# A state space stage whose output rotation goes from VectorE to GpSimd

## The chip, the core and the metric

One core of a Trainium2 chip runs the whole program. The metric is the device time of one execution in microseconds; where several runs are given, their median. Beside the times there is one profiled execution of the same kernel, and all rows below come from it.

## The reference

The program computes two transformer-like blocks one after the other on a sequence of 256 tokens of width 2048, in f32. The change touches one part of the second block, the state space layer:

```python
def s5_ssm(u, a_re, a_im, log_dt, b_re, b_im, c_re, c_im, d_skip):
    # 32 groups of 16 channels, 64 complex states for each group
    bu_re = jnp.einsum('gph,blgh->blgp', bb_re, ug)
    bu_im = jnp.einsum('gph,blgh->blgp', bb_im, ug)
    # combine: complex product of a decay and a state, plus the new input
    _, _, xs_re, xs_im = lax.associative_scan(combine, (a_re_t, a_im_t, bu_re, bu_im), axis=1)
    y = (jnp.einsum('ghp,blgp->blgh', c_re, xs_re)
         - jnp.einsum('ghp,blgp->blgh', c_im, xs_im)
         + d_skip.reshape(SSM_GROUPS, SSM_GROUP) * ug)
```

The result goes through a gelu, a gated linear unit and a branch product, and is merged with a windowed attention branch through sigmoid gates.

## The kernel before

**Weight products.** Nearly all of the time goes into products of a stationary weight tile with 256 tokens. Each f32 weight is split into a high part (ScalarE, L379) and a low part (VectorE, L473: raw minus high), and TensorE multiplies high by high, high by low and low by high (L670, L671, L672). A chunk is four weight tiles of 128x256, 512 KB; a ring of four chunks holds raw, high and low parts. SyncE loads chunk c when the low part of chunk c-4 is made; ScalarE and VectorE make chunk c's parts when TensorE is done with chunk c-4 and the load has landed; TensorE takes 24 matmuls for a chunk. A unit of four chunks fills one PSUM bank, which VectorE evacuates (L543 in this stage) before the unit after next is due; ScalarE then applies the sigmoid (L433).

**The state space stage.** It runs while TensorE computes the 40 chunks of the gates (phase `ps`). A complex state decays by its magnitude and turns by its angle at each token. The kernel takes the turning out: it multiplies the input by a table of rotations (the cosines `er` and sines `ei` of `s_tab`), runs a real scan with the magnitude alone, and rotates the scanned states back. The states are worked in four quarters `q` of four tiles, each quarter in two halves `p` of two tiles, so eight halves of 128x512 elements for a real and an imaginary part (`xr`, `xi`). For each half VectorE in `StateSpace.dve` does, in this order:

- input rotation, L2502 to L2510: four multiplies of a table (SBUF) with the product that TensorE left in PSUM (`work`), one add, one subtract (both inputs in SBUF);
- four scans of 128x256, L2514 (two inputs in SBUF);
- output rotation, L2521 to L2528: four multiplies, one subtract and one scalar_tensor_tensor, all in SBUF, with temporaries `tq`, `sq` and `ta`; the last one computes `-q3 - q1`, the negated imaginary part, which the output product needs.

Between these steps stand calls of `split()`. Each makes as many low splits of gate chunks as are due by its count (`4 * EACH * calls // 64`, with eight calls a half), so that TensorE gets weights in step. After the first half of quarters 1 to 3 VectorE also adds the skip term to the output of the quarter before (`output`, L2460), for which it waits for TensorE's output sum.

**TensorE in the stage.** Before certain chunks it computes the inputs of a half (`inputs`, before chunks 9q-1 and 9q+2) or the output sum of a quarter (`outputs`, L2438, 16 matmuls, before chunk 9q+13; the last one after chunk 39). `outputs(q)` waits for `made`, which VectorE raises after a quarter's second output rotation. The next table load into the same slot waits for that output sum, as do the scans that overwrite its states.

**GpSimd.** Its queue is one list: tables of the state space in the first block (`StateTables.pool_factors`, `pool_tables`), low parts and sums of squares of the phases, then two instructions for the attention (`window.pool`), then the later phases. The output matrix `gi` of the tables is the imaginary part that multiplies `xi`.

The order on each engine is written out by hand; no planner moves anything.

Of the kernel before, what the change touches and what calls it, by code (L numbers as in the profile page):

```python
# [22 lines left out]
ALU = mybir.AluOpType  # L23
# [3 lines left out]
T = 256  # L27
# [38 lines left out]
QT = ST // 4  # L66
# [124 lines left out]
class Stream:  # L191
# [402 lines left out]
    def pool(self, eng, phs):  # L594
        for ph in phs:
            if ph.k.pool:
                def step(v, j, ph=ph):
                    self.pool_finish(eng, ph, v, (ph.base["u"] + j) % 2)
                self.loop(eng, ph, step)
# [1349 lines left out]
class StateTables:  # L1949
# [71 lines left out]
    def pool_factors(self, eng):  # L2021
        link, em, sqs, s = self.link, self.em, self.sqs, self.s
        tt, ts = eng.tensor_tensor, eng.tensor_scalar
        abr, abi, zr, zi, t1, den = self.abr, self.abi, self.zr, self.zi, self.t1, self.den
        are, aim = s.par("are"), s.par("aim")
        eng.memset(self.tab[:, :, S5_C:S5_M], 0.0)
        eng.wait_ge(self.waves, 1)
        eng.wait_ge(self.inverse, 1)
        eng.tensor_copy(em[:, 0, 0, :], self.co[:])
        link(eng.tensor_copy(em[:, 0, 1, :], self.si[:]))  # L2030
        for n in range(7):
            c, sn = em[:, n, 0, :], em[:, n, 1, :]
            tt(sqs[:, 0, :], c, c, ALU.mult)
            tt(sqs[:, 1, :], sn, sn, ALU.mult)
            link(tt(em[:, n + 1, 1, :], c, sn, ALU.mult))
            tt(em[:, n + 1, 0, :], sqs[:, 0, :], sqs[:, 1, :], ALU.subtract)
            link(ts(em[:, n + 1, 1, :], em[:, n + 1, 1, :], 2.0, None, ALU.mult))
        tt(abr[:], self.mag[:], self.co[:], ALU.mult)
        link(tt(abi[:], self.mag[:], self.si[:], ALU.mult))
        link(ts(abr[:], abr[:], -1.0, None, ALU.add))  # L2040
        for z, x, y, op in ((zr, abr, abi, ALU.add), (zi, abi, abr, ALU.subtract)):
            tt(z[:], x[:], are, ALU.mult)
            link(tt(t1[:], y[:], aim, ALU.mult))
            link(tt(z[:], z[:], t1[:], op))
            link(tt(z[:], z[:], den[:], ALU.mult))
        eng.wait_ge(self.loaded, 32)
        zrw, ziw = spread(zr[:], 16), spread(zi[:], 16)
        for g, x, y, op in ((self.gr, self.cr, self.ci, ALU.subtract), (self.gi, self.ci, self.cr, ALU.add)):
            tt(g[:], x[:], zrw, ALU.mult)
            link(tt(self.tmp[:], y[:], ziw, ALU.mult))  # L2050
            link(tt(g[:], g[:], self.tmp[:], op))

    def pool_tables(self, eng, half):
        link, em, w1, w2 = self.link, self.em, self.w1, self.w2
# [299 lines left out]
class StateSpace:  # L2354
# [5 lines left out]
    def __init__(self, dram, s, ua, pa, gates, window, states, tab, xr, xi, bq, sem):  # L2360
        self.dram, self.s, self.ua, self.pa, self.gates, self.window = dram, s, ua, pa, gates, window
        self.states, self.tab, self.xrs, self.xis, self.bq = states, tab, xr, xi, bq
        self.q1, self.q2, self.q3 = s.tq[:], s.sq[:], s.ta[:]
        self.inputs_in = [sem("even_inputs_loaded"), sem("odd_inputs_loaded")]
        self.tables_in = [sem("even_states_loaded"), sem("odd_states_loaded")]
        (self.lk, self.bu, self.bu_read, self.made, self.summed, self.mixed, self.gelu, self.high,
         self.low) = (sem("space_" + n) for n in (
             "vector_link", "bu_ready", "bu_read", "ready", "outputs_summed", "outputs_mixed", "gelu_ready",
             "outputs_high", "outputs_low"))

    def bank(self, i):
# [56 lines left out]
        ins.then_inc(self.bu, 1)  # L2428

    def outputs(self, eng, q):  # L2430
        eng.wait_ge(self.made, q + 1)
        if q < 2:
            eng.wait_ge(self.window.low, q + 3)
        at_least(eng, self.mixed, q - 1)
        for b in range(QT):
            for im, xs in ((0, self.xrs[q % 2]), (1, self.xis[q % 2])):
                at = S5_C + (im * QT + b) * P
                ins = eng.matmul(self.ybank(q), self.tab[:, q % 2, at:at + P], xs[:, b, :],  # L2438
                                 start=b + im == 0, stop=b == QT - 1 and im == 1)
        ins.then_inc(self.summed, 1)  # L2440
# [10 lines left out]
    def dve_last(self, eng):  # L2451
# [3 lines left out]
        eng.tensor_tensor(s.a0[:, 0:4, 1, :], self.ua[:, S2:S2 + 4, :], s.a0[:, 0:4, 0, :].bitcast(F32),  # L2455
                          ALU.subtract).then_inc(self.low, 1)

    def output(self, eng, q):
        eng.wait_ge(self.summed, q + 1)
        eng.scalar_tensor_tensor(out=self.ua[:, S2 + q, :], in0=self.ua[:, S2 + q, :], scalar=self.s.par("d2", q),  # L2460
                                 in1=self.ybank(q), op0=ALU.mult, op1=ALU.add).then_inc(self.mixed, 1)

    def dve(self, eng, previous):
        s, gates = self.s, self.gates
        link = Link(eng, self.lk)
        tt, stt = eng.tensor_tensor, eng.scalar_tensor_tensor
        q1, q2, q3 = self.q1, self.q2, self.q3
        chunks = gates.units * gates.nc
        done, calls = [0], [0]

        def one():

            v, k = divmod(done[0], gates.nc)
            s.split_low(eng, gates, v, v, k)
            if k == gates.nc - 1:
                if v:
                    s.evacuate(eng, gates, v - 1, (gates.base["u"] + v - 1) % 2)
                else:
                    s.evacuate(eng, previous, previous.units - 1, (gates.base["u"] - 1) % 2)
            done[0] += 1  # L2480

        def split():

            calls[0] += 1
            while done[0] < min(chunks, self.LEAD + 4 * self.EACH * calls[0] // 64):
                one()

        for _ in range(self.LEAD):
            one()
        for q in range(4):  # L2490
            er, ei = (self.tab[:, q % 2, S5_E + k * QT * T:S5_E + (k + 1) * QT * T].rearrange("p (a t) -> p a t", a=QT)
                      for k in range(2))
            xr, xi = self.xrs[q % 2], self.xis[q % 2]
            eng.wait_ge(self.tables_in[q % 2], 16 * (q // 2 + 1))
            for p in range(2):
                split()
                eng.wait_ge(self.bu, 2 * q + p + 1)
                if q > 1 and p == 0:
                    eng.wait_ge(self.summed, q - 1)
                pr = slice(2 * p, 2 * p + 2)  # L2500
                re, im = (self.bank(2 * p + i).rearrange("p (a t) -> p a t", a=2) for i in range(2))
                tt(q1, er[:, pr], re, ALU.mult)  # L2502
                link(tt(q2, ei[:, pr], im, ALU.mult))  # L2503
                split()
                link(tt(xr[:, pr], q1, q2, ALU.add))  # L2505
                tt(q1, er[:, pr], im, ALU.mult)
                split()
                tt(q2, ei[:, pr], re, ALU.mult).then_inc(self.bu_read, 1)
                eng.wait_ge(self.bu_read, 2 * q + p + 1)
                link(tt(xi[:, pr], q1, q2, ALU.subtract))  # L2510
                split()
                for jl in range(2 * p, 2 * p + 2):
                    for xs in (xr, xi):
                        ins = eng.tensor_tensor_scan(  # L2514
                            xs[:, jl, :], self.tab[:, q % 2, S5_M + jl:S5_M + jl + 1].to_broadcast([P, T]),
                            xs[:, jl, :], 0.0, ALU.mult, ALU.add)
                    if jl % 2 == 0:
                        split()
                link(ins)
                split()  # L2520
                tt(q1, er[:, pr], xr[:, pr], ALU.mult)  # L2521
                tt(q3, ei[:, pr], xr[:, pr], ALU.mult)  # L2522
                link(tt(q2, ei[:, pr], xi[:, pr], ALU.mult))  # L2523
                split()
                link(tt(xr[:, pr], q1, q2, ALU.subtract))
                link(tt(q1, er[:, pr], xi[:, pr], ALU.mult))
                split()
                ins = stt(out=xi[:, pr], in0=q3, scalar=-1.0, in1=q1, op0=ALU.mult, op1=ALU.subtract)  # L2528
                if p == 0:
                    link(ins)  # L2530
                    if q:
                        self.output(eng, q - 1)
                else:
                    ins.then_inc(self.made, 1)
                    eng.wait_ge(self.made, q + 1)
        while done[0] < chunks:
            one()


def feed_forwards(nc, dram, s, a1, fo, raw, out_dram, states):  # L2540
    with ExitStack() as st:
# [68 lines left out]
        with nc.Block() as block:  # L2610
# [60 lines left out]
            def _(eng):  # L2671
# [7 lines left out]
                s.pool(eng, ffn[6:])  # L2679
                tables.stores_done(eng)  # L2680
                window.pool(eng)
                s.pool(eng, phs)

            @block.tensor
# [221 lines left out]
```

## Time and profile before

| | us |
|---|---|
| median of 3 runs (lowest, highest) | 2882.45 (2881.48, 2887.85) |
| span of the profiled execution | 2882.9 |
| TensorE busy | 2802.8 (97%) |
| VectorE busy | 1823.4 (63%) |
| ScalarE busy | 1245.7 (43%) |
| GpSimd busy | 396.0 (14%) |

The profile gives the span from the first to the last instruction; the execution's own time is not given beside it, and the span stands for it. Busy shares are averages over stages with different limits, so the rows for single stretches matter more. A matmul's end is modelled: its row shows 0.28 us while the next one starts 0.11 us after it. A time in a row of the timeline counts from the start of the span.

### The profile page before, as it was taken

To read this page: it belongs to the slowest core of one execution; us is meant where nothing else is said; L and a number is where in the kernel's file an instruction comes from. 1 tells how busy PE (TensorE), PEld (TensorE's weight loads), DVE (VectorE), ACT (ScalarE), POOL (GpSimd) and SP (SyncE) were. 2 spreads that over 40 slices of the span, in tenths; PEclk is the share of its full clock that TensorE was granted. 3 is DMA by queue.
4 is the path that set the end of the run, shared out by engine and by line. 5 is a ranking of instruction groups with operands and counts; after the bars stand their busy time and mean duration, and the time that the engine had idled before them with its cause. 6 is when DMAs were issued, how large, how long until landed. Compare 5 with 4: busy or idle time off the path is not lost.

```text
span 2882.9 us, 61146 instructions
## 1 busy us (share of the span) xinstructions
PE 2802.8 (97%) x24650; PEld 2752.2 (95%) x24650; DVE 1823.4 (63%) x2175; ACT 1245.7 (43%) x1511; POOL 396.0 (14%) x549
## 2 busy tenths in 40 slices
PE   8999699999999999999999999999999999999998
PEld 8999687999989999999999999998999999999998
DVE  6678747775435655655555668697667655665664
ACT  5355223544334543444434545434454443443444
POOL 0000230110002139300461210000110000010011
PEclk9999899999999999999999999999999999999999
DMA  6654002566635566666667565554555665556564
GB/s 235 195 192 147 16 31 88 191 189 204 190 102 164 190 197 190 219 213 189 197 194 236 191 195 163 193 196 157 193 192 189 197 192 193 193 188 199 184 198 149
DMA packets 138418, 514.10 MB, mean 178 GB/s; under 512 B 15360, under 2 KB 15616, under 8 KB 136960
## 3 DMA queue, kind: packets, MB, share of 16 engines
q1 hardware_dynamic: 138240, 511.58, 54.9%
q8 instruction: 129, 2.11, 0.3%
q14 instruction: 49, 0.40, 0.0%
HBM read 503.12 MB, written 8.40 MB: 177 GB/s over the span
## 4 chain that ended last, share of the span: by engine, by line
PE 64%; DVE 4%; issue 1%; ACT 1%; DVEq 0%; ACTq 0%
PE acc L670 21%; PE acc L671 21%; PE acc L672 21%; DVE lo L473 1%; PE work L2170 0%; ACT hi L379 0%; DVE s_xr L2514 0%; PE acc L2203 0%; DVE tb L543 0%; DVE sq L2523 0%; DVE ua L2514 0%; DVE ub L2514 0%; DVE s_xr L2505 0%; DVE sq L2503 0%; DVE ta L2522 0%
## 5 line engine op out<-in xcount | busy, mean ns | idle before, releaser
L670 PE MATMUL acc<-a,hi 128*128 128x256 f32 x5504 | 1527.0, 277 | 16.3 <-DVE lo L473 14.5
L671 PE MATMUL acc<-a,hi 128*128 128x256 f32 x5504 | 1521.5, 276 | 0.0
L672 PE MATMUL acc<-a,lo 128*128 128x256 f32 x5504 | 1521.4, 276 | 0.0
L473 DVE TENSOR_TENSOR lo<-qx,hi 128x1024 fp32r<-128x1024 f32 x704 | 896.4, 1290 | 674.6 <-ACT hi L379 672.9
L670 PEld LDWEIGHTS acc<-a,hi 128*128 128x128 f32 x5504 | 1035.3, 188 | 20.5 <-issue 14.8
L671 PEld LDWEIGHTS acc<-a,hi 128*128 128x128 f32 x5504 | 1035.3, 188 | 0.8 <-issue 0.5
L672 PEld LDWEIGHTS acc<-a,lo 128*128 128x128 f32 x5504 | 1035.3, 188 | 0.0
L379 ACT ACTIVATE hi<-qx 128x1024 fp32r<-128x1024 f32 x704 | 733.9, 1057 | 646.4 <-PE acc L672 629.0
L620 POOL TENSOR_TENSOR a<-th,a 128x512 f32 (+1 forms) x64 | 84.9, 1327 | 1381.2 <-ACT a L424 1381.1
L473 DVE TENSOR_TENSOR lo_x<-next_raw,hi_x 128x1024 fp32r<-128x1024 f32 x128 | 162.2, 1281 | 115.0 <-ACT hi_x L379 115.0
L670 PE MATMUL acc<-a,hi_in 128*128 128x256 f32 x768 | 215.4, 280 | 9.8 <-DVE lo_in L473 9.8
L670 PE MATMUL acc<-a,hi_x 128*128 128x256 f32 x768 | 215.8, 281 | 5.8 <-DVE lo_x L473 5.8
L672 PE MATMUL acc<-a,lo_in 128*128 128x256 f32 x768 | 213.8, 278 | 0.0
L671 PE MATMUL acc<-a,hi_in 128*128 128x256 f32 x768 | 213.8, 278 | 0.0
L671 PE MATMUL acc<-a,hi_x 128*128 128x256 f32 x768 | 212.8, 277 | 0.0
L672 PE MATMUL acc<-a,lo_x 128*128 128x256 f32 x768 | 212.8, 277 | 0.0
L379 ACT ACTIVATE hi_x<-next_raw 128x1024 fp32r<-128x1024 f32 x128 | 133.9, 1058 | 144.2 <-PE acc L672 94.9
L473 DVE TENSOR_TENSOR lo_in<-raw_in,hi_in 128x1024 fp32r<-128x1024 f32 x96 | 115.4, 1222 | 68.2 <-ACT hi_in L379 68.1
L670 PEld LDWEIGHTS acc<-a,hi_in 128*128 128x128 f32 x768 | 146.1, 190 | 11.2 <-DVE lo_in L473 9.7
L670 PEld LDWEIGHTS acc<-a,hi_x 128*128 128x128 f32 x768 | 144.9, 189 | 8.5 <-issue 5.8
L671 PEld LDWEIGHTS acc<-a,hi_in 128*128 128x128 f32 x768 | 146.0, 190 | 0.3 <-issue 0.2
L672 PEld LDWEIGHTS acc<-a,lo_in 128*128 128x128 f32 x768 | 145.9, 190 | 0.0
(503 smaller groups left out, 2779.2 us busy)
## 6 DMA issues: line engine op xcount, KB each, us to landing
qx<-in_ffn SPq DMA_DIRECT2D x256, 512.0 KB, 4.2
raw_in<-in_w_in SPq DMA_DIRECT2D x96, 512.0 KB, 4.3
qx<-in_w_in SPq DMA_DIRECT2D x92, 512.0 KB, 3.7
qx<-in_up_gate SPq DMA_DIRECT2D x88, 512.0 KB, 4.2
qx<-in_up_val SPq DMA_DIRECT2D x88, 512.0 KB, 4.3
qx<-in_down SPq DMA_DIRECT2D x88, 512.0 KB, 4.2
next_raw<-in_wq SPq DMA_DIRECT2D x32, 512.0 KB, 4.3
next_raw<-in_wk SPq DMA_DIRECT2D x32, 512.0 KB, 4.3
```

The lines of the kernel that those rows point to most:

```text
L379: eng.activation(self.hi[:, slot, :], self.raw[:, slot, :], ACT.Copy).then_inc(self.s_hi, 1)
L473: eng.tensor_tensor(self.lo[:, slot, :], self.raw[:, slot, :], self.hi[:, slot, :].bitcast(F32), ALU.subtract).then_inc(self.s_lo, 1)
L620: eng.tensor_tensor(out[:, :, 1, :], self.th[:, s], out[:, :, 0, :].bitcast(F32), ALU.subtract).then_inc(self.s_pool, 1)
L670: eng.matmul(out, self.hi[:, slot, cols], a[:, 0, :], start=opens, stop=False)
L671: eng.matmul(out, self.hi[:, slot, cols], a[:, 1, :], start=False, stop=False)
L672: ins = eng.matmul(out, self.lo[:, slot, cols], a[:, 0, :], start=False, stop=closes)
```

## The change

The output rotation of seven halves moves to GpSimd. A new `StateSpace.pool`, placed in GpSimd's queue behind the attention's two instructions, waits for a half's scans (`scanned`), rotates in place and raises `turned`. The eighth half is rotated by VectorE, behind its last two `split()` calls. The new `turn` holds six instructions: four multiplies (two into temporaries, two in place), a subtract and an add. GpSimd's temporaries are `sq2` and `ta`, VectorE's `tq` and `sq`. The imaginary part is no longer negated; instead `gi` is multiplied by -1 once, when the tables are made. TensorE's output sum waits for `turned` (two for each quarter; for the last one 7, and `made` of VectorE). VectorE no longer waits for `made` in its loop, has six `split()` calls a half and 50 in all, and the divisor goes from 64 to 50.

```diff
@@ StateTables.pool_factors
             link(tt(g[:], g[:], self.tmp[:], op))
+        link(ts(self.gi[:], self.gi[:], -1.0, None, ALU.mult))
@@ StateSpace.__init__
-        self.q1, self.q2, self.q3 = s.tq[:], s.sq[:], s.ta[:]
+        self.q1, self.q2 = s.tq[:], s.sq[:]
+        self.p1, self.p2 = s.sq2[:], s.ta[:]
@@ StateSpace.outputs
-        eng.wait_ge(self.made, q + 1)
+        if q < 3:
+            eng.wait_ge(self.turned, 2 * q + 2)
+        else:
+            eng.wait_ge(self.turned, 7)
+            eng.wait_ge(self.made, 1)
@@ new in StateSpace
+    def turn(self, eng, link, q, p, v1, v2):
+        er, ei = self.factors(q)
+        pr = slice(2 * p, 2 * p + 2)
+        xr, xi = self.xrs[q % 2][:, pr], self.xis[q % 2][:, pr]
+        tt = eng.tensor_tensor
+        tt(v1, ei[:, pr], xr, ALU.mult)
+        tt(v2, ei[:, pr], xi, ALU.mult)
+        tt(xr, er[:, pr], xr, ALU.mult)
+        link(tt(xi, er[:, pr], xi, ALU.mult))
+        tt(xr, xr, v2, ALU.subtract)
+        return tt(xi, xi, v1, ALU.add)
+
+    def pool(self, eng):
+        link = Link(eng, self.plk)
+        for n in range(7):
+            eng.wait_ge(self.scanned, n + 1)
+            self.turn(eng, link, n // 2, n % 2, self.p1, self.p2).then_inc(self.turned, 1)
+            eng.wait_ge(self.turned, n + 1)
@@ StateSpace.dve
-            while done[0] < min(chunks, self.LEAD + 4 * self.EACH * calls[0] // 64):
+            while done[0] < min(chunks, self.LEAD + 4 * self.EACH * calls[0] // 50):
...
-                link(ins)
+                ins.then_inc(self.scanned, 1)
                 split()
-                tt(q1, er[:, pr], xr[:, pr], ALU.mult)
-                tt(q3, ei[:, pr], xr[:, pr], ALU.mult)
-                link(tt(q2, ei[:, pr], xi[:, pr], ALU.mult))
-                split()
-                link(tt(xr[:, pr], q1, q2, ALU.subtract))
-                link(tt(q1, er[:, pr], xi[:, pr], ALU.mult))
-                split()
-                ins = stt(out=xi[:, pr], in0=q3, scalar=-1.0, in1=q1, op0=ALU.mult, op1=ALU.subtract)
-                if p == 0:
-                    link(ins)
-                    if q:
-                        self.output(eng, q - 1)
-                else:
-                    ins.then_inc(self.made, 1)
-                    eng.wait_ge(self.made, q + 1)
+                if p == 0 and q:
+                    self.output(eng, q - 1)
+        eng.wait_ge(self.scanned, 8)
+        split()
+        split()
+        self.turn(eng, link, 3, 1, q1, q2).then_inc(self.made, 1)
@@ GpSimd's queue
                 window.pool(eng)
+                space.pool(eng)
                 s.pool(eng, phs)
```

## Rows read from the trace of the kernel before

**Rows 1.** The page, part 1: busy us (share of the span) xinstructions.

```profile
PE 2802.8 (97%) x24650; PEld 2752.2 (95%) x24650; DVE 1823.4 (63%) x2175; ACT 1245.7 (43%) x1511; POOL 396.0 (14%) x549
```

**Rows 2.** Busy us by engine in the stage: start:end, length, engines, granted clock.

```profile
1835.00:1973.00 138.00, 130.89 (x1045) 126.59 (x1044) 129.88 (x176) 47.46 (x66) 0.00 (x0) 1.00 0.52 169
```

**Rows 3.** Waits of TensorE, 1831 to 1980: us in total, times, longest.

```profile
PE acc L670 <- DVE lo L473: 7.1, 8, 1.3
```

**Rows 4.** Timeline of TensorE: start us, us, instruction, idle time before.

```profile
1870.99 0.28 PE L672 MATMUL acc<-a,lo 128*128 128x256 f32 x1
1872.08 0.36 PE L670 MATMUL acc<-a,hi 128*128 128x256 f32 x1 [0.82 <-DVE lo L473]
1872.28 0.28 PE L671 MATMUL acc<-a,hi 128*128 128x256 f32 x1
```

**Rows 5.** Timeline of VectorE, first output rotation to the next split.

```profile
1847.78 0.68 DVE L2521 TENSOR_TENSOR tq<-s_tab,s_xr 128x512 f32<-128x512 f32 x1
...
1851.16 1.23 DVE L473 TENSOR_TENSOR lo<-qx,hi 128x1024 fp32r<-128x1024 f32 x1
```

**Rows 6.** Groups of VectorE, 1831 to 1973: count, busy us, mean ns, idle before.

```profile
L473 DVE TENSOR_TENSOR lo<-qx,hi 128x1024 fp32r<-128x1024 f32 x38 | 46.4, 1221 | 7.8 <-ACT hi L379 7.0
L2514 DVE TENSOR_TENSOR_SCAN s_xr<-s_tab,s_xr 128x256 f32<-128x256 f32 x16 | 10.9, 680 | 0.1
...
L2528 DVE SCALAR_TENSOR_TENSOR ub<-ta,tq 128x512 f32<-128x512 f32 x4 | 2.7, 683 | 0.0
```

**Rows 7.** Groups of GpSimd, whole span.

```profile
L614 POOL TENSOR_TENSOR sq<-sq,tq 128x512 f32<-128x512 f32 x27 | 35.2, 1305 | 231.5 <-ACT tq L421 231.5
```

**Rows 8.** Timeline of GpSimd and VectorE, a table step in the first block.

```profile
1111.45 1.04 POOL L2069 TENSOR_TENSOR t_w<-t_tab,t_em 128x512 f32<-128x512 f32 x1
1112.05 1.52 DVE L473 TENSOR_TENSOR lo<-qx,hi 128x1024 fp32r<-128x1024 f32 x1 [1.28 <-ACT hi L379]
1112.45 2.02 POOL L2070 TENSOR_TENSOR t_w<-t_tab,t_em 128x512 f32<-128x512 f32 x1
1113.49 0.68 DVE L496 TENSOR_TENSOR x<-acc,x 128x512 f32 x1
1114.55 1.30 POOL L2071 TENSOR_TENSOR t_tab<-t_w 128x512 f32<-128x512 f32 x1
1114.77 2.16 DVE L473 TENSOR_TENSOR lo<-qx,hi 128x1024 fp32r<-128x1024 f32 x1 [0.59 <-ACT hi L379]
...
1119.88 1.29 POOL L2074 TENSOR_TENSOR t_tab<-t_w 128x512 f32<-128x512 f32 x1
```

**Rows 9.** Timeline of VectorE: first instruction of the halves 4 and 6.

```profile
1889.92 0.68 DVE L2502 TENSOR_TENSOR tq<-s_tab,work 128x512 f32<-128x512 f32 x1
...
1923.07 0.68 DVE L2502 TENSOR_TENSOR tq<-s_tab,work 128x512 f32<-128x512 f32 x1
```

**Rows 10.** Timeline of VectorE, end of the last output rotation.

```profile
1971.30 0.68 DVE L543 TENSOR_TENSOR tb<-acc,rstd 128x512 f32<-128x512 f32 x1
1971.90 0.68 DVE L2528 SCALAR_TENSOR_TENSOR ua<-ta,tq 128x512 f32<-128x512 f32 x1
```

**Rows 11.** The chain that ended last, by time: TensorE's last output sum.

```profile
1974.61 3.45 PE acc L2438 x16
```

**Rows 12.** Half 4's rotation begins; second output sum; TensorE's waits 1835 to 1908.

```profile
1899.34 0.69 DVE L2521 TENSOR_TENSOR tq<-s_tab,s_xr 128x512 f32<-128x512 f32 x1
1908.17 0.59 PE L2438 MATMUL acc<-s_xr,s_tab 128*128 128x256 f32 x2
PE acc L670 <- DVE lo L473: 2.0, 2, 1.2
```

**Rows 13.** Timeline of GpSimd in the first block.

```profile
1087.00 0.74 POOL L2051 TENSOR_TENSOR t_gi<-t_gi,t_tmp 128x256 f32<-128x256 f32 x1
...
1213.57 1.30 POOL L620 TENSOR_TENSOR a<-th,a 128x512 f32 x1 [9.60 <-ACT a L424]
```

**Rows 14.** Busy us by engine behind the stage, columns as in rows 2.

```profile
2055.00:2065.00 10.00, 8.18 (x58) 7.98 (x58) 7.96 (x9) 4.90 (x6) 2.83 (x2) 0.84 0.50 184
```

**Rows 15.** Groups of ScalarE, 1831 to 1973.

```profile
L433 ACT ACTIVATE ub<-tb,prm 128x256 f32<-128x256 f32 x18 | 8.2, 503 | 79.4 <-DVE tb L543 79.4
```

More of the change, by code:

```diff
@@ L2362, in __init__ @@
         self.states, self.tab, self.xrs, self.xis, self.bq = states, tab, xr, xi, bq
-        self.q1, self.q2, self.q3 = s.tq[:], s.sq[:], s.ta[:]
+        self.q1, self.q2 = s.tq[:], s.sq[:]
+        self.p1, self.p2 = s.sq2[:], s.ta[:]
         self.inputs_in = [sem("even_inputs_loaded"), sem("odd_inputs_loaded")]
         self.tables_in = [sem("even_states_loaded"), sem("odd_states_loaded")]
-        (self.lk, self.bu, self.bu_read, self.made, self.summed, self.mixed, self.gelu, self.high,
-         self.low) = (sem("space_" + n) for n in (
-             "vector_link", "bu_ready", "bu_read", "ready", "outputs_summed", "outputs_mixed", "gelu_ready",
+        (self.lk, self.plk, self.bu, self.bu_read, self.scanned, self.turned, self.made, self.summed, self.mixed,
+         self.gelu, self.high, self.low) = (sem("space_" + n) for n in (
+             "vector_link", "pool_link", "bu_ready", "bu_read", "scanned", "turned", "last_turned", "outputs_summed", "outputs_mixed", "gelu_ready",
              "outputs_high", "outputs_low"))
@@ L2456, in dve_last, with factors @@
                           ALU.subtract).then_inc(self.low, 1)
+    def factors(self, q):
+        return (self.tab[:, q % 2, S5_E + k * QT * T:S5_E + (k + 1) * QT * T].rearrange("p (a t) -> p a t", a=QT)
+                for k in range(2))
+    def turn(self, eng, link, q, p, v1, v2):
[15 more added lines that the diff above has]
+            eng.wait_ge(self.turned, n + 1)
     def output(self, eng, q):
@@ L2466, in dve @@
         tt, stt = eng.tensor_tensor, eng.scalar_tensor_tensor
-        q1, q2, q3 = self.q1, self.q2, self.q3
+        q1, q2 = self.q1, self.q2
         chunks = gates.units * gates.nc
@@ L2490, in dve @@
         for q in range(4):
-            er, ei = (self.tab[:, q % 2, S5_E + k * QT * T:S5_E + (k + 1) * QT * T].rearrange("p (a t) -> p a t", a=QT)
-                      for k in range(2))
+            er, ei = self.factors(q)
             xr, xi = self.xrs[q % 2], self.xis[q % 2]
```

## The prediction

> **What bounds the kernel now.** I began with the page: TensorE is busy 97% of the span and GpSimd 14% [rows 1], so a gain can come only where TensorE waits. The busy times by stretch then show the state space stage of the second block as the odd one: from 1835 to 1973 us VectorE is busy 129.9 of 138 us, TensorE 130.9, GpSimd never, at full clock [rows 2]. The waits of TensorE in that stage are one kind: for the low part of a weight chunk, which VectorE makes, 7.1 us in 8 waits [rows 3]. No wait there ends on a transfer or on ScalarE. So VectorE bounds the stage, by little.
>
> The 7.1 us understates the loss. A gap is counted from the modelled end of the last matmul, 0.28 us after its start, while running matmuls start every 0.11 us. Around the first stall the starts are 1.09 and 0.20 us apart instead of 0.11 and 0.11: 1.07 us lost where the wait says 0.82 [rows 4]. At 0.25 us more for each of eight, the stage loses 7.1 + 2.0 = 9.1 us. This is the ceiling of the gain here.
>
> **What the change removes from VectorE.** Seven of eight output rotations, six instructions each. The first five of one take 1851.16 - 1847.78 = 3.38 us start to start [rows 5]; the sixth has the same form, mean 0.68 [rows 6]. Together 4.06 us, seven times: 28.4 us. The other work stays: 36 low splits, 32 scans, the input rotation. The new divisor, 50, fits the six split calls that a half now has (6 x 8 + 2), so the splits stay evenly spread, 4.3 a half against 4.5.
>
> **What it adds to GpSimd.** 42 multiplies, subtracts and adds of 128x512 f32. One alone takes 1.30 us [rows 7]; GpSimd has nothing else in the stage [rows 2]. Six of exactly this kind, two multiplies and a sum twice over, took 1121.17 - 1111.45 = 9.7 us beside VectorE, links included [rows 8]. So a rotation takes about 10 us where a half takes 16.6: two halves are 1923.07 - 1889.92 = 33.15 us apart [rows 9]. GpSimd keeps up; 7 x 10 = 70 us of work in about 130.
>
> **What GpSimd's work costs VectorE.** This is the term that decides. In [rows 8] a low split (both inputs in SBUF) that starts at 1114.77 beside a GpSimd op from 1114.55 lasts 2.16 us, not 1.22 [rows 6], and ends 1.08 us after that op. The other way round, the GpSimd op of 1112.45 ends at 1114.47, 0.90 us after the split of 1112.05 ended at 1113.57. They take turns. The VectorE op of 1113.49, which reads PSUM, runs in its usual 0.68 us beside the same GpSimd op. So a GpSimd op costs VectorE 2.16 - 1.22 = 0.94 us, say 0.9, if it falls before an instruction with two SBUF inputs (splits, scans, both sums of the input rotation), and nothing if VectorE reads PSUM or idles.
>
> The Trainium skill says the same under "SBUF — State Buffer", section "Who interferes with whom": the second read interface of VectorE is GpSimd's only one, and whoever comes first keeps it for the whole instruction; the trace agrees, by the 2.16 us. Taken at its word for every one of the 42, it would charge 42 x 1.30 = 54.6 us and put the time near 2907.
>
> All 42 charged at 0.9 are 37.8 us. What can hide them: in a stage of 138 us VectorE idles 8.1 us [rows 2] and reads PSUM in 32 input multiplies and 10 evacuations (about 0.6 us each from start to start, 25 us) and three output sums (about 1 us): some 35 us, spread evenly. GpSimd works 70 of 130 us, so 35 x 70/130 = 19 us of them lie inside its work. Charged: 37.8 - 19 = 19 us. The ends are 0 (everything falls well) and 37.8 (nothing does); I take 19 since both engines queue without pause and the order of their instructions is fixed.
>
> **The sum.** VectorE now ends its last rotation at 1971.90 + 0.68 = 1972.6 [rows 10], 137.6 us after 1835. New: 137.6 - 28.4 + 19 = 128.2, so 1963.2. TensorE starts the last output sum at 1974.6 [rows 11]; without the 9.1 us it would want it at 1965.5. VectorE is 2.3 us ahead: TensorE bounds the stage again, and the 9.1 us come back.
>
> From them goes one new wait. TensorE's output sum of a quarter needs two rotations from GpSimd. Behind it in TensorE's queue stand all weight chunks; behind its result, VectorE's output sum and so every later split. The scans of the fourth half end at 1899.3 [rows 12]. VectorE can run ahead only by the ring of four chunks, so I put that 2.5 to 4.5 us earlier, 1895 to 1897; plus 10 us that is 1905 to 1907. TensorE took it up by 1908.2 and had waited 2.0 us in two waits in front of it, 2.5 with what the count leaves out: it wants it at 1905.6 [rows 12]. Late by up to 1.5 us, I take 0.5; the same a quarter later; nothing at the first, which has the long start of the stage in front of it. So 1.1 us in all, bounds 0 and 4. Gain: 9.1 - 1.1 = 8.0 us.
>
> The rest costs nothing. The sign is one more GpSimd instruction (its neighbours on that table, 128x256, take 0.74 us [rows 13]) in a first block where GpSimd sat idle about 9.6 us before each piece of work [rows 13]; if that cover were gone it would hold back a low split by under 1 us, once. The two extra temporaries are buffers that nothing else uses in the stage. No DMA is moved; table loads still follow the output sums. At the end the last rotation now stands whole behind the last split: 4.1 us plus 0.6 for the evacuation where TensorE needs 2.7 for its last chunk. While VectorE is 2.3 us ahead this is covered; with VectorE the bound it costs 2 us. A thing I can't set: near 2060 the clock was granted at half for a few us after a gap [rows 14], which cost about 1.7 us; everything behind the stage moves, and that may go or a like one come.
>
> The profiled execution spans 2882.9 us, 0.4 above the median; I take the gain from the median: 2882.45 - 8.0 = 2874.5.
>
> **Rivals.**
> 1. *VectorE stays the bound, or the new wait is longer.* Where GpSimd's charge is 24 to 30 us, or the output sums wait their 4 us, only part of the 9.1 comes back: with 26, VectorE ends at 1970.2 and TensorE starts the output sum with it, 4.4 us earlier than before: 2878.0. For it: the splits and the scans are more than half of what VectorE keeps, so GpSimd may meet them more often than evenly. Against: the first three GpSimd ops in [rows 8] cost VectorE 0.30 us (1.52 - 1.22), nothing and 0.94 us, a mean of 0.41, below the 19/42 = 0.45 of my sum. This would read as within 0.2%.
> 2. *The turn-taking eats the saving.* All 37.8 us charged: 137.6 - 28.4 + 37.8 = 147.0, last rotation at 1982.0, where TensorE started at 1974.6: 7.4 us later, 2889.9. It decides from a charge of 30.4 us on, 0.72 us for each op on the mean. For it: the exclusive turns are plain in the rows. Against: 35 us of the stage are open to GpSimd without cost.
> 3. *The change does its work but TensorE was not held by VectorE alone.* ScalarE's high part waits for VectorE's evacuations (79.4 us of its idle time [rows 15]) and then makes several chunks in a row; closer evacuations may leave VectorE waiting for it in new places. VectorE has these pauses already, and GpSimd's reads fall into them. It would cost at most the 2.3 us of lead first: 2876 to 2879.
>
> **How the numbers follow.** Of this kernel a measurement can tell some 0.2%, 5.8 us, from no change. Full or nearly full return (gain of 6 to 10 us): 0.58. Rivals 1 and 3, with gains of 5.8 down to a loss as small: 0.32 (0.22 and 0.10). Rival 2: 0.10. So faster 0.58, same 0.32, slower 0.10. The range goes from the ceiling with a lost half clock (9.1 + 1.7, and a little for the spread of runs: 2870.5) into the losses of rival 2 only as far as 8 in 10 needs: 2883.0. The likeliest case alone holds 2871 to 2877.
>
> **What would show it.** Right: TensorE's waits for the low part in the stage nearly gone; VectorE's busy time there lower by some 10 us (28.4 less 19, since a blocked instruction counts as busy); low splits and scans that last 0.5 to 0.9 us longer beside GpSimd; GpSimd busy 65 to 75 us; the stage shorter by 8 us and all behind it as before. Wrong: splits lengthened so often that VectorE is busy without a pause and TensorE still waits for it (rivals 1 and 2), or TensorE waiting at its output sums for GpSimd for over 2 us each.

## The result, and the profile after

The changed kernel takes 2879.11 us (median of 15 runs, 2877.0 to 2880.78); the kernel before, beside it on the same chips, 2884.86 us (15 runs, 2881.48 to 2887.85). The ratio is 0.9981, with a 95% interval of 0.9974 to 0.9988: 5.5 us less by the ratio, where 8.0 us (0.9972) were forecast and 9.1 us were held to be the ceiling. The interval leaves no doubt of a gain, but its size lies just inside what I had called no change (0.2%). The profiled execution agrees: its span fell from 2882.9 to 2877.8 us.

The busy times of the stage after the change, columns as in [rows 2], over 133 us instead of 138:

```profile
1835.00:1968.00 133.00, 129.24 (x1044) 125.97 (x1043) 122.71 (x135) 50.03 (x66) 75.76 (x42) 1.00 0.56 178
```

GpSimd now works 75.8 us there, where 70 were reckoned, in its 42 instructions; VectorE is down to 122.7 us, and has idle time of 10.3 us. TensorE's waits in the stage, which answer to [rows 3] (us in total, times, longest):

```profile
PE acc L2444 <- POOL ub L2478: 2.1, 2, 1.6
PE acc L2444 <- POOL ua L2478: 1.4, 1, 1.4
PE acc L670 <- DVE lo L473: 0.3, 1, 0.3
```

The waits for the low part are gone but for 0.3 us. In their place TensorE waits 3.5 us at output sums (L2444) for the last instruction of a GpSimd rotation (L2478). From start to start of the matmuls, the measure by which the old waits came to 9.1 us in the prediction, the three waits cost 0.6, 1.5 and 1.8 us. Here is the second one, in GpSimd's and VectorE's timelines and TensorE's row behind it:

```profile
1896.43 1.30 POOL L2473 TENSOR_TENSOR sq<-s_tab,s_xr 128x512 f32<-128x512 f32 x1 [4.90 <-DVE ua L2542]
1897.69 2.26 POOL L2474 TENSOR_TENSOR ta<-s_tab,ua 128x512 f32<-128x512 f32 x1
1899.91 2.27 POOL L2475 TENSOR_TENSOR s_xr<-s_tab,s_xr 128x512 f32<-128x512 f32 x1
1902.15 1.28 POOL L2476 TENSOR_TENSOR ua<-s_tab,ua 128x512 f32<-128x512 f32 x1
1903.51 1.63 POOL L2477 TENSOR_TENSOR s_xr<-s_xr,ta 128x512 f32<-128x512 f32 x1
1905.09 2.25 POOL L2478 TENSOR_TENSOR ua<-ua,sq 128x512 f32<-128x512 f32 x1
```

```profile
1897.05 3.98 DVE L473 TENSOR_TENSOR lo<-qx,hi 128x1024 fp32r<-128x1024 f32 x2 [0.76 <-ACT hi L379]
1900.96 0.68 DVE L2530 TENSOR_TENSOR tq<-s_tab,work 128x512 f32<-128x512 f32 x1
1901.55 0.67 DVE L2531 TENSOR_TENSOR sq<-s_tab,work 128x512 f32<-128x512 f32 x1
1902.26 1.72 DVE L2533 TENSOR_TENSOR s_xr<-tq,sq 128x512 f32<-128x512 f32 x1
1904.01 0.69 DVE L2534 TENSOR_TENSOR tq<-s_tab,work 128x512 f32<-128x512 f32 x1
1904.62 1.60 DVE L473 TENSOR_TENSOR lo<-qx,hi 128x1024 fp32r<-128x1024 f32 x1
```

```profile
1907.39 0.48 PE L2444 MATMUL acc<-s_xr,s_tab 128*128 128x256 f32 x1 [1.36 <-POOL ua L2478]
```

In these rows GpSimd's second and third multiply last 2.26 and 2.27 us, beside two low splits that together take 3.98 us instead of 2.4. Its fourth lasts 1.28 us: VectorE reads PSUM then (L2531), and only the add behind it (L2533, both inputs in SBUF) is held up, to 1.72 us. The rotation takes 1907.34 - 1896.43 = 10.9 us, and TensorE starts 0.05 us after it.

What VectorE paid stands in its groups, which answer to [rows 6] (count, busy us, mean ns, idle time before):

```profile
L473 DVE TENSOR_TENSOR lo<-qx,hi 128x1024 fp32r<-128x1024 f32 x45 | 64.7, 1448 | 13.4 <-ACT hi L379 12.9
L2533 DVE TENSOR_TENSOR s_xr<-tq,sq 128x512 f32<-128x512 f32 x8 | 12.0, 1500 | 0.1
L2542 DVE TENSOR_TENSOR_SCAN s_xr<-s_tab,s_xr 128x256 f32<-128x256 f32 x16 | 10.9, 681 | 0.1
L2530 DVE TENSOR_TENSOR tq<-s_tab,work 128x512 f32<-128x512 f32 x8 | 5.4, 676 | 0.0
L2538 DVE TENSOR_TENSOR ua<-tq,sq 128x512 f32<-128x512 f32 x4 | 5.2, 1297 | 0.1
L2538 DVE TENSOR_TENSOR ub<-tq,sq 128x512 f32<-128x512 f32 x4 | 4.4, 1094 | 0.1
```

Against their length without GpSimd (1.221 us for a split, 0.69 for an add or subtract) the splits are longer by 45 x 0.227 = 10.2 us, L2533 by 8 x 0.81 = 6.5, L2538 by 4 x 0.61 + 4 x 0.40 = 4.0. Together 20.7 us, 0.49 for each of the 42 GpSimd instructions; 19 us, or 0.45, were reckoned. L2530, which reads PSUM, has its old length, and so have the scans, of which the prediction expected otherwise: in this trace GpSimd had ended each rotation at least 0.6 us before the next half's scans began.

### The profile page after: what moved, and what is told of

Read it like the earlier page. It is cut to its first block, busy times and chain, and to the rows that moved or that the text cites. A ratio compares the mean times of both kernels' runs of the same rounds, so it can differ in the third digit from the quotient of the medians.

```text
span 2877.8 us, 61137 instructions
## 1 busy us (share of the span) xinstructions
PE 2797.8 (97%) x24650; PEld 2748.5 (96%) x24650; DVE 1817.3 (63%) x2133; ACT 1246.5 (43%) x1511; POOL 475.4 (17%) x592
## 4 chain that ended last, share of the span: by engine, by line
PE 64%; DVE 4%; issue 1%; ACT 1%; DVEq 0%; ACTq 0%
PE acc L670 21%; PE acc L671 21%; PE acc L672 21%; DVE lo L473 2%; DVE s_xr L2533 0%; PE work L2171 0%; ACT hi L379 0%; DVE s_xr L2542 0%; PE acc L2204 0%; DVE ua L2538 0%; DVE tb L543 0%; DVE sq L2536 0%; DVE ub L2538 0%; DVE tq L2530 0%; DVE sq L2531 0%
## 5 line engine op out<-in xcount | busy, mean ns | idle before, releaser
L473 DVE TENSOR_TENSOR lo<-qx,hi 128x1024 fp32r<-128x1024 f32 x704 | 907.0, 1306 | 675.0 <-ACT hi L379 673.8
L670 PEld LDWEIGHTS acc<-a,hi 128*128 128x128 f32 x5504 | 1034.9, 188 | 12.1 <-issue 10.9
```

The source lines that it names most:

```text
L473: eng.tensor_tensor(self.lo[:, slot, :], self.raw[:, slot, :], self.hi[:, slot, :].bitcast(F32), ALU.subtract).then_inc(self.s_lo, 1)
L670: eng.matmul(out, self.hi[:, slot, cols], a[:, 0, :], start=opens, stop=False)
```

## The experiments

Of each the stage is given as the profiled run has it: from TensorE's first input product to its last output sum. It was 142.96 us before (1831.49 to 1974.45) and is 138.11 us in the changed kernel (1831.27 to 1969.38), 4.85 less. All ratios are to the kernel before, run beside; its own median lay between 2883.5 and 2885.1 us beside the different runs, so kernels are compared by their ratios and stages, not by their times alone.

**Output sums one chunk later.**

```diff
-            if c == self.EACH * q + 13:
+            if c == self.EACH * q + 14:
```

> The changed kernel with one edit: TensorE takes the output sum of a quarter before chunk 9q+14 instead of 9q+13, so GpSimd has one chunk (2.7 us) more for the two rotations that it needs. Theory A (what is lost of the ceiling is only GpSimd's latency, 0.6, 1.5 and 1.8 us at three sums, since a rotation takes 11 us beside VectorE): TensorE's waits for GpSimd vanish, no wait takes their place, 3 to 4 us less than the changed kernel's 2879.1: about 2875.5, ratio to before 0.9968. Rival B (VectorE, charged by turn-taking, is as late as TensorE): TensorE waits for the low part instead, gain over the changed kernel under 1.5 us: 2877.6 to 2879.

2878.46 us, ratio 0.9978 (0.9969 to 0.9987); stage 138.17 us, no shorter than the changed kernel's. TensorE's waits:

```profile
PE acc L670 <- DVE lo L473: 3.4, 5, 1.2
```

The waits for GpSimd are gone to the last, and as many us of waits for the low part have come. Theory A, that only GpSimd's latency was missing, is wrong; rival B holds. In the changed kernel the rotations' end and VectorE's own pace stood at one height, and only the first showed in the waits.

**Output sums two chunks later** (`+ 15` in the same place).

> The same with chunk 9q+15. Theory A: TensorE waits for nothing here either, but VectorE's wait for the output sum (which it adds behind the first half of the next quarter) comes late and holds the splits: within 1 us of the run with 9q+14, or up to 3 us slower. Rival B: no difference from 9q+13 or 9q+14.

2886.24 us (median of nine runs; a tenth took 8898.6 us), ratio 1.0003 (0.9993 to 1.0012); stage 143.52 us. VectorE's and TensorE's waits:

```profile
DVE ua L2489 <- PE acc L2444: 9.3, 3, 4.3
```

```profile
PE acc L670 <- DVE lo L473: 7.2, 8, 2.2
```

Now VectorE waits 9.3 us for the output sums that it adds to the skip term (L2489), with the splits queued behind. Theory A foresaw this wait, but not its size: nearly 8 us over the run with `+ 14`, where at most 3 were expected. In the traces 5.4 us of it are in the stage and 1.7 behind it, where TensorE's clock fell near 2063 us in this run and not in the other.

**No rotations in seven halves.** GpSimd only raises the semaphore; the states of these halves go into the output sums unrotated.

```diff
-            self.turn(eng, link, n // 2, n % 2, self.p1, self.p2).then_inc(self.turned, 1)
+            eng.memset(self.p1[:, 0, 0:1], 0.0).then_inc(self.turned, 1)
```

> The changed kernel with the output rotations of seven halves left out: GpSimd only raises the semaphore. No latency, no turn-taking; VectorE's work as in the changed kernel. Theory A: TensorE is the bound throughout the stage, so this is the ceiling of the change: 9.1 to 9.5 us less than before, 4 us less than the changed kernel, about 2875; VectorE's low splits all last 1.22 us. Rival B (something else than VectorE held TensorE in part): less than 7 us under before.

2873.81 us, ratio 0.9963 (0.9950 to 0.9977); stage 133.31 us. (The five times lie in two groups, 2873.0 to 2873.8 and 2877.3 to 2877.8; the trace is of one of the second, so the stage is the better measure here.) TensorE does not wait once between 1831 and 1967:

```profile
1835.00:1968.00 133.00, 133.00 (x1072) 130.11 (x1072) 107.09 (x139) 53.63 (x71) 0.69 (x7) 1.00 0.57 189
```

This is the ceiling: 142.96 - 133.31 = 9.65 us in the stage. The prediction had 9.1 from the waits and the gaps between matmul starts. By the ratio this kernel is 10.7 us faster than the one before (6.6 to 14.4), which agrees.

**The latency alone.** The seven rotations again left out, and in their place 19 memsets in a row that only write.

```diff
-            self.turn(eng, link, n // 2, n % 2, self.p1, self.p2).then_inc(self.turned, 1)
+            for m in range(18):
+                link(eng.memset(self.p1, 0.0))
+            eng.memset(self.p1, 0.0).then_inc(self.turned, 1)
```

> The changed kernel with the seven rotations left out and in their place 19 GpSimd memsets of 128x512, which read nothing: about 11 us from the end of the scans to the semaphore, as long as a rotation takes, but no turn-taking over reads. With the run without rotations (no latency, no turn-taking: the ceiling) and the one with 9q+14 (turn-taking, no latency: 0.6 us gained of 5) this is the third corner. Theory A (the turn-taking holds VectorE back and so makes the scans late; the latency alone would fit): VectorE's low splits last 1.22 us again, TensorE waits for GpSimd under 1.5 us in all, 2.5 to 5 us less than the changed kernel, 2874 to 2877. Rival B (the latency by itself costs what was missing): TensorE waits for GpSimd 3.5 us as before, 2878 to 2880. Should memsets take turns with VectorE as well, its splits will show it.

2873.52 us, ratio 0.9964 (0.9952 to 0.9977); stage 133.31 us, that of the ceiling to the last digit. One stand-in for a rotation in GpSimd's timeline, and the splits in VectorE's groups:

```profile
1861.75 10.46 POOL L2485 MEMSET sq<- 128x512 f32 x18 [2.57 <-DVE ub L2544]
1872.27 0.53 POOL L2486 MEMSET sq<- 128x512 f32 x1
```

```profile
L473 DVE TENSOR_TENSOR lo<-qx,hi 128x1024 fp32r<-128x1024 f32 x46 | 55.6, 1219 | 19.0 <-ACT hi L379 18.5
```

From 1861.75 to 1872.80 are 11.05 us, as long as a rotation took, and no output sum waits for it. The splits last 1.219 us, and VectorE has 18.5 us of idle time before them, waiting for ScalarE's high parts. So latency without turn-taking costs nothing, and turn-taking with more time for the latency (`+ 14`) costs all that was missing. What keeps the change from its ceiling is the turn-taking over SBUF reads, by way of VectorE: it makes the scans end later, and from there the 11 us become too long. The last scan of the fourth half, in the changed kernel and here, in stages that began at 1831.27 and 1831.59:

```profile
1895.62 0.67 DVE L2542 TENSOR_TENSOR_SCAN ua<-s_tab,ua 128x256 f32<-128x256 f32 x1
```

```profile
1890.32 0.67 DVE L2544 TENSOR_TENSOR_SCAN ua<-s_tab,ua 128x256 f32<-128x256 f32 x1
```

It ends 5.3 us earlier without the turn-taking.

**The turn-taking priced by itself.** The kernel before, its rotations kept on VectorE, with 42 GpSimd multiplies beside them whose result nobody uses.

```diff
+    def pool(self, eng):
+        c, v = self.s.consts[:, 0:2 * T].rearrange("p (a t) -> p a t", a=2), self.s.sq2[:]
+        for h in range(7):
+            eng.wait_ge(self.lk, 15 * (h // 2) + 8 * (h % 2) + 4)
+            for n in range(6):
+                ins = eng.tensor_tensor(v, c, c, ALU.mult)
+                ins.then_inc(self.plk, 1)
+                eng.wait_ge(self.plk, 6 * h + n + 1)
...
                 window.pool(eng)
+                space.pool(eng)
```

> The kernel before, its own rotations kept on VectorE, and beside them 42 GpSimd multiplies of 128x512 f32 on the constants, six behind the scans of each of seven halves, whose result nobody uses. It prices the turn-taking by itself, in a stage where VectorE is the bound. Theory A: each costs VectorE on the mean 0.4 to 0.6 us: 42 x 0.5 = 21 us, and nearly all of it reaches the end: 15 to 25 us slower than before, 2898 to 2909; more than in the changed kernel, since VectorE's own rotations have two inputs in SBUF too. Rival C (the two engines hardly disturb one another, and the stretched instructions hide elsewhere): under 6 us slower.

2916.33 us, ratio 1.0109 (1.0094 to 1.0125), 31 us slower; the stage is 173.97 us, 31.0 longer. The direction was right, the size beyond the expected range. The costliest groups of VectorE:

```profile
L473 DVE TENSOR_TENSOR lo<-qx,hi 128x1024 fp32r<-128x1024 f32 x41 | 57.2, 1397 | 10.5 <-ACT hi L379 9.7
L2532 DVE TENSOR_TENSOR ta<-s_tab,s_xr 128x512 f32<-128x512 f32 x8 | 11.4, 1421 | 0.0
L2535 DVE TENSOR_TENSOR s_xr<-tq,sq 128x512 f32<-128x512 f32 x8 | 10.3, 1289 | 0.1
```

Here the stage grows by 31.0 us, 0.74 for each of the 42 instructions. Summed over VectorE's groups as above, the splits (7.2) and the rotation's first five (24.4) are 31.6 us longer, 0.75 each against 0.49 in the changed kernel, so nearly all of it reaches the end. TensorE's clock also fell here in its long waits; as VectorE's longer instructions alone make up the 31 us, that seems to have cost nothing more:

```profile
1835.00:1970.00 135.00, 112.87 (x828) 108.38 (x827) 128.44 (x138) 38.69 (x53) 53.19 (x36) 0.94 0.43 144
```

The likely difference to the changed kernel is the neighbour: behind the scans this VectorE runs its own rotation, which reads only SBUF, where the changed one goes on to input multiplies that read PSUM. No run varies that alone.

**The same, one step earlier** (the wait's `+ 4` becomes `+ 3`), so that GpSimd meets the scans. One run.

> The kernel before with the 42 unused GpSimd multiplies again, but each group of six is let go one step earlier, behind the input rotation, so that it meets the four scans. In all traces so far the scans had ended before GpSimd began, so whether a scan (two inputs in SBUF, one of them a repeated column) takes turns with GpSimd is unseen. Theory A (a scan counts as two inputs): scans beside GpSimd last about 1.5 us instead of 0.67, some two or three of each four. Rival: scans stay at 0.67 us and GpSimd's ops at 1.3 us beside them; the stage is then 5 to 10 us shorter than with the later start.

2918.06 us, stage 174.34 us, no shorter than with the later start. The scans in VectorE's groups:

```profile
L2524 DVE TENSOR_TENSOR_SCAN s_xr<-s_tab,s_xr 128x256 f32<-128x256 f32 x16 | 18.8, 1173 | 0.1
L2524 DVE TENSOR_TENSOR_SCAN ub<-s_tab,ub 128x256 f32<-128x256 f32 x8 | 11.7, 1460 | 0.0
```

A scan takes turns too, as theory A had it: a group's mean is up to 1.46 us instead of 0.67. So in the changed kernel scans keep their 0.68 us because GpSimd has finished one rotation before the next scans begin.

**The eighth half on GpSimd too.** The loop in `pool` runs over eight, VectorE's last rotation goes, and every output sum waits for `turned` at 2q + 2.

```diff
-        if q < 3:
-            eng.wait_ge(self.turned, 2 * q + 2)
-        else:
-            eng.wait_ge(self.turned, 7)
-            eng.wait_ge(self.made, 1)
+        eng.wait_ge(self.turned, 2 * q + 2)
...
-        for n in range(7):
+        for n in range(8):
...
-        self.turn(eng, link, 3, 1, q1, q2).then_inc(self.made, 1)
```

> The changed kernel with the eighth half on GpSimd too. VectorE loses its last 3.8 us, but the last output sum then waits for a rotation that begins behind the last scans. In the changed kernel these end at 1961.1 or so and TensorE takes the sum at 1969.4. Theory A (a GpSimd rotation takes 7 us without and up to 11 us with neighbours): it ends at 1968 to 1971, TensorE waits 0 to 2 us more: within 2 us of the changed kernel. Rival (the last rotation on VectorE is what saves the end): over 3 us slower.

2883.27 us, ratio 1.000 (0.9991 to 1.001): by the times the whole gain is lost, and the rival is right. TensorE's waits for GpSimd rise from 3.5 to 5.4 us:

```profile
PE acc L2440 <- POOL ua L2474: 3.3, 2, 2.0
PE acc L2440 <- POOL ub L2474: 2.1, 2, 1.6
```

The new wait of 2.0 us ends at 1972.5, and behind it the granted clock of TensorE falls to its lower level (1.2 GHz) for about a third of the next 10 us (in the changed kernel it stays up there):

```profile
1970.00:1980.00 10.00, 8.02 (x41) 6.90 (x40) 6.88 (x6) 5.72 (x10) 2.44 (x2) 0.83 0.54 149
```

The traces explain only a part of the loss. The stage is 140.32 us, 2.2 over the changed kernel and still 2.6 under the kernel before. The clock adds next to nothing between the two traces: from the last output sum to the end it is 908.7 us here and 908.5 in the changed kernel, whose clock falls near 2057 instead, where it stays up here. What makes up the rest of the difference in the times stays open.

**ScalarE's order.** In the stage ScalarE did the sigmoid of a unit, for which it waits for VectorE's evacuation, ahead of the next unit's high parts [rows 15]. Here it comes behind the second chunk of the unit after next, in the kernel before, in the changed one, and in that with `+ 14`.

```diff
-                    s.act_split(eng, ps, v, v)
+                    for k in range(ps.nc):
+                        s.act_chunk(eng, ps, v, v, k)
+                        if k == 1 and v > 1:
+                            s.act_finish(eng, ps, v - 2, (ps.base["u"] + v - 2) % 2)
...
-                    if v:
-                        s.act_finish(eng, ps, v - 1, (ps.base["u"] + v - 1) % 2)
+                s.act_finish(eng, ps, ps.units - 2, (ps.base["u"] + ps.units - 2) % 2)
```

> The kernel before with one edit on ScalarE: the sigmoid of a unit is done behind the second chunk of the unit after next instead of ahead of its first, so that ScalarE no longer holds back the high parts until VectorE has evacuated. In the stage VectorE stood idle for the high part 7 to 8 us. Theory A (VectorE bounds the stage before, so its idle time is the loss): most of these 7 us come back, 4 to 7 us less than before: ratio 0.9976 to 0.9986. Rival (the idle time is the ring's: VectorE would wait for TensorE's release of the slot anyway): no change, within 1.5 us.

In the kernel before: 2881.52 us, ratio 0.9992 (0.9983 to 1.0001), stage 140.94 us. Less than the 4 to 7 us expected and not told apart from no change by the times; in the trace the stage is 2.0 us shorter.

> The same edit in the changed kernel. There TensorE waits only at the output sums for GpSimd. Theory A (what is left is GpSimd's latency, 11 us from the end of the scans): VectorE's scans end earlier by what the idle time gives, 1 to 3 us less than the changed kernel. Rival (VectorE fills the gaps with instructions that meet GpSimd, so rotations take longer): no change or slower by up to 2 us.

In the changed kernel: 2877.72 us, ratio 0.9978 (0.9968 to 0.9987), stage 135.90 us, 2.2 less than the changed kernel's, as theory A expected; the ratios of the two kernels (0.9978 and 0.9981) are not told apart. From 1831 to 1980 TensorE waits for GpSimd once over 0.2 us:

```profile
PE acc L2444 <- POOL ua L2478: 1.3, 1, 1.3
PE acc L670 <- DVE lo L473: 0.3, 1, 0.3
```

> Both edits in the changed kernel: ScalarE's order and the output sum one chunk later. With 9q+14 alone the waits for GpSimd were gone, but 3.4 us of waits for the low part came back, so VectorE and GpSimd's latency were level. Theory A (two bounds at the same height, each hiding the other): only both edits together reach the ceiling of the run without rotations, 3 to 5 us less than the changed kernel: ratio to before about 0.9965. Rival (turn-taking alone fills VectorE): not below the run with 9q+14 alone by more than 1 us.

Both edits: 2876.95 us, ratio 0.9977 (0.9967 to 0.9987), stage 135.31 us, 2.8 less than the changed kernel's and 2.0 more than the ceiling. Its time is the lowest of the kernels that do the whole computation, but its interval overlaps with that of the changed kernel (0.9974 to 0.9988): that it beats it is shown by the stage in the traces, not by the ratio. The ceiling, which theory A expected both edits to reach, is missed, and ScalarE's order alone had given 2.2 of the 2.8 us. The rest of the distance is VectorE: TensorE's only waits in the stage are for its low parts, and VectorE is busy 126.3 us of 133 here, 107.1 without rotations.

```profile
PE acc L670 <- DVE lo L473: 1.4, 2, 1.0
```

## Why the prediction was right, and where its size was off

The prediction gave 2874.5 us in a range of 2870.5 to 2883.0; 2879.11 were measured. Of the 4.6 us between, 2.4 lie in the starting point: it took the median of three runs, 2882.45, where fifteen give 2884.86. (That a span of 2882.9 lay 0.4 above the median was a sign of it: the changed kernel's profiled execution took 2879.62 us with a span of 2877.8.) The rest is the gain, 5.5 us instead of 8.0. So the range held, but the likeliest case, a gain of 6 to 10 us at 0.58, did not come; the result fell among the gains under 5.8 us, which had 0.32.

- *What bounds the stage*: right. Without rotations TensorE runs without a wait and the stage loses 9.65 us; 9.1 were read from the waits plus the hidden part of each gap, where the waits alone would have given 7.1.
- *What is removed, what GpSimd does, the sign, the temporaries*: right as far as the traces tell: the stage begins at 1831.27 us instead of 1831.49, and from the last output sum to the end it is 908.46 us instead of 908.43.
- *The charge by turn-taking*: right in kind, 19 us reckoned, 20.7 measured. The size owes something to luck: the working subtracts 19 us of VectorE's free time one for one from 37.8 us of charge, a step that no run tests; had it let off the share of GpSimd's instructions that falls on free time (19 of 70 us), the same 37.8 would have left 27 to 28. Its far end, all 42 charged at 0.9 (37.8), was not reached even beside VectorE's own rotation (31.6), and still less the 54.6 us of charging each in full. Rival 2, slower by 7.4 us, did not come: it needed a charge of 30.4.
- *The lead of VectorE*: too large. The last rotation was to end at 1963.2 and ended at 1967.7. The charge accounts for 1.7 us of that; idle time, reckoned as hiding a part of GpSimd's work and left at 8.1 us, was 10.3. That VectorE is held by the ring while TensorE waits would explain the longer idle time; it is not shown apart.
- *The new wait*: the step that was mis-sized. "I take 0.5; the same a quarter later; nothing at the first", 1.1 us in all with 0 and 4 as bounds; it measured 1.5, 1.8 and 0.6, 3.9 us in all. The times around it were met: scans of the fourth half to end at 1895 to 1897 (1896.3), TensorE to want the sum at 1905.6 (1905.9, its start less 1.5). What failed is the length of a rotation: 9.7 us were read beside a VectorE that runs a split every 2.7 us, and taken as "about 10"; next to this denser VectorE the seven take 10.8 to 11.1 (10.9 before the second sum), and at the sums that wait all of the excess is late. With 11 the same working gives 1.4 at the second sum. The run of memsets shows what stands behind it: with the same 11 us but no turn-taking the scans end 5.3 us earlier and nothing waits, so the wait is there only together with the charge. The sum then closes: 9.65 less 3.9, less 0.5 for the one low-part wait left (0.3 and its hidden part), is 5.25 against 4.85 in the stage.
- *Rival 1* (VectorE stays the bound, or the new wait is longer), with 2878.0, is nearest to the measured time. Its second half came (3.9 us of its 4); its first, a charge of 24 to 30 us, did not, yet the run with `+ 14` shows VectorE's pace close behind GpSimd's latency. That the two would stand level, so that more time for GpSimd alone gains nothing, was in none of the cases.

One thing that the prediction left open: near 2060, behind a TensorE gap of 1.8 us, the clock falls to its lower level in both traces (and in those with `+ 15` and without rotations), and the time from the last output sum to the end is 908.4 to 908.5 us. In five others (`+ 14`, the three with ScalarE's order, the memsets) the same gap is there and the clock stays up, and the same work takes 906.7 to 906.9 us. The changed kernel and the one with ScalarE's order and `+ 14`:

```profile
2055.00:2065.00 10.00, 9.18 (x66) 9.21 (x67) 7.51 (x8) 4.73 (x6) 1.30 (x1) 0.83 0.61 215
```

```profile
2050.00:2060.00 10.00, 8.23 (x73) 8.06 (x72) 7.61 (x8) 6.05 (x7) 2.39 (x2) 1.00 0.67 225
```

So 1.7 us hang on whether the clock follows that gap, as reckoned. The traces of before and after both have the fall, so it is no part of the 4.85 us between their stages, but it blurs any comparison of times by as much.

## What to carry to other kernels

In this stage, moving SBUF arithmetic from VectorE to GpSimd relieved VectorE by the moved time less half a microsecond for each GpSimd instruction of 128x512, and beside more VectorE work on SBUF such an instruction cost three quarters. Put GpSimd's work where VectorE reads PSUM, and size its latency from the moved work's real neighbours, not from a quieter stretch. When a wait goes and a new one of nearly the size of what is missing appears, lift it alone before believing it: here the next bound stood level, and only taking out the turn-taking, with the latency kept, showed the cause.

## What the runs showed of the hardware

- A scan (128x256 f32, its first input one repeated column) is held up by GpSimd like an op with two full inputs: 0.67 us alone, up to 1.46 on the mean of a group beside GpSimd's multiplies.
- GpSimd memsets of 128x512, 0.53 us each, took no time from VectorE: splits 1.219 us beside 70 us of them. The Trainium skill says so too ("SBUF — State Buffer", "Who interferes with whom": a GpSimd instruction that only writes is not contended with by a VectorE instruction with two SBUF inputs), and the trace agrees.
- GpSimd's multiply of 128x512 lasts 1.30 us alone and 2.27 us between low splits; where both had such work queued, as from 1897 to 1902 us in the changed kernel, the two engines went by turns, one instruction each.
